# A transformer layer with a mixture of experts: slot table by one-hot matmuls, expert rows added to the residual by accumulating transfers

## The chip, the cores and the metric

The kernel runs on one core of one Trainium2 chip. The metric is the device time of one execution in microseconds (us). Three timed runs of the kernel before gave 2468.05, 2471.11 and 2472.49 us, with a median of 2471.11.

## The reference, cut to what matters

One layer over 2048 latent tokens of width 1024 and 256 context tokens: modulation, a token mixer (recurrence and windowed attention), a residual and layer norm that give `x`, and then the part that the change touches:

```python
h_lat = modulate(x, sh2, sc2).reshape(B * S, D)
y = hier_moe(h_lat, router_g, router_gb, router_e, router_eb, w1, w3, w2)
x = layer_norm(ALPHA * x + g2 * y, ln2_g, ln2_b)

def hier_moe(xf, ...):                         # top-1 of 4 groups, top-2 of its 8 experts
    gate = softmax(top_v) * p_g                # two gates for each token
    flat_e = expert_id.reshape(-1)             # 4096 assignments over 32 experts
    pcounts = (counts + 127) // 128 * 128      # each expert gets whole blocks of 128 slots
    dest = pstarts[sorted_e] + position        # the slot of each assignment
    xb = x_pad[slot_tok].reshape(n_blocks, 128, D)
    yb = (silu(xblk @ w1[e]) * (xblk @ w3[e])) @ w2[e]     # for each block
    return segment_sum(yb[dest] * gate, tok_sorted)
```

Everything is float32. With these inputs 31 experts are used, in 50 blocks.

## The kernel before

The kernel is eight stages, one after the other, each a block of code in which every engine has its own instruction stream, ordered by semaphores; a stage begins when all engines have left the one before. The last four are output (which writes the residual rows `x1_d` and the modulated rows `h2_d` to DRAM), routing, experts and combine.

**Routing** (`phase_route`, from L1395). The router's logits of all 16 token tiles lie in SBUF as 128 x 576. VectorE finds the group and the two experts of each token with `max` and `max_index`, tile by tile (L1433, L1434, L1445, L1446), builds one-hot rows, TensorE sums them to counts and ranks (L1536, L1537), and VectorE derives the slot of each of the 4096 assignments (`slot_i`, L1475), the list of experts in use (L1492) and the tables that steer the expert loop (L1481 to L1511). Each instruction waits for the one before it on a semaphore (`link`). To turn "slot of an assignment" into "token of a slot", GpSimd issues 32 indirect transfers of 128 token numbers each to a DRAM table, `slot_tok_d` (L1547). SyncE then reads the table back (L1563), TensorE transposes it (L1539) and VectorE writes it to SBUF as `gidx`, one column for each block (L1524). SyncE starts the first expert's weights as soon as the expert list is there (L1391).

**Experts** (`phase_experts`, from L1566). For each block of 128 slots: GpSimd copies a column of `gidx` to `ix` (L1642), gathers 128 rows of `h2_d` by an indirect transfer (L1645) and waits until they have landed; TensorE transposes them, multiplies by w1 and w3 and, one block later, by w2 (L1814 to L1816, three half-precision products for each float32 one). For each new expert SyncE loads 6 MB of weights in six pieces of 1 MB through one staging area (L1391), ScalarE rounds each piece to its high half (L1661, L1667) and VectorE subtracts to get its low half (L1734). VectorE scales the block's result by `g2` into the single buffer `y0` (`scale_y`, L1770), and ScalarE stores it to `y_d`, by a transfer placed one step later in its stream (`store_y`, L1688):

```python
def scale_y(n):
    dve.wait_ge(y_mm, START + n + 1)
    dve.wait_ge(y_st, START + 16 * n)      # the store before has landed
```

TensorE's second product of block n waits for `scale_y` of block n - 1. Last, SyncE writes zeros to the unused blocks of `y_d` (L1630).

**Combine** (`phase_combine`, from L1871). For each of the 16 token tiles, with two buffers: GpSimd copies two columns of `slot_i` and gathers the tile's two rows from `y_d` (L1905, L1909); ScalarE multiplies `x1` by ALPHA (L1934, L1939); VectorE adds the two gated rows (L1960, L1961), takes mean and variance (L1962 to L1967), applies the norm in two full-width steps (L1968, L1972) around a `pow` that GpSimd computes (L1915), and ScalarE stores the tile (L1931). VectorE waits for each of its own instructions on a semaphore before the next.

Of the kernel before, what the change touches and what calls it, by code (L numbers as in the profile page):

```python
# [8 lines left out]
F16 = mybir.dt.float16  # L9
# [6 lines left out]
P = 128  # L16
# [25 lines left out]
NG = 4  # L42
# [14 lines left out]
TAB_NB, TAB_NB1, TAB_NB2, TAB_NR, TAB_FREE, TAB_NR1 = 224, 225, 226, 227, 228, 229  # L57
# [14 lines left out]
e_ssv e_pw_s e_a_tr e_o_mm e_o_act e_v e_pw e_h_tr e_h_ev e_r_mm e_lg f_ld f_v f_act f_mm f_tr g_st_ld0  # L72
g_st_ld1 g_st_ld2 g_st_ld3 g_st_ld4 g_st_ld5 g_hi13 g_lo13 g_hi2 g_lo2 g_g2_ld g_x_ix g_x_tr g_x_hi g_x_lo
g_up_mm g_silu g_h g_h_tr g_h_hi g_h_lo g_y_mm g_y_ev g_y_st g_zero g_z_st h_ld h_ix h_v h_pw h_a_x h_mh
h_x_ld0 h_x_ld1 h_o_st0 h_o_st1
# [13 lines left out]
def hybrid_layer(nc, x, c2, w_mod, b_mod, w_in, rg_par, lam, rg_wa, rg_wx, ctx_x, sink, w_out, gn, ln1, router, router_b,  # L89
                 w1, w3, w2, ln2, cos_t, sin_t, ident, masks, tri, iota, tok_id, out):  # L90
    with ExitStack() as stack:
# [20 lines left out]
        x1_d = dram("x1_d", [SEQ, D])  # L112
        h2_d = dram("h2_d", [SEQ, D])
        slot_tok_d = dram("slot_tok_d", [64 * P, 1], I32)
        y_d = dram("y_d", [64 * P, D])
# [4 lines left out]
        slot_i = sb("slot_i", [P, 2 * T_LAT], I32)  # L120
        gates = sb("gates", [P, 2 * T_LAT])
        blk_tab = sb("blk_tab", [1, TAB_SIZE], I32)
        gidx = sb("gidx", [P, 66], I32)
# [48 lines left out]
def phase_modulation(nc, env):  # L172
# [10 lines left out]
    zi = small[0:64, 128:256].bitcast(I32)  # L183
# [5 lines left out]
    with nc.Block() as block:  # L189
        @block.sync  # L190
        def _(sp):
# [15 lines left out]
            sp.wait_ge(rows_st, 32)  # L207
# [31 lines left out]
        def _(dve):  # L239
            nc.vector.memset(zi, 0).then_inc(rows_done, 1)  # L240
# [1154 lines left out]
def phase_route(nc, env):  # L1395
# [5 lines left out]
    names = [("logits", T * 36), ("pad8", T * 8), ("gm8", T * 8), ("gi8", T * 8), ("gif", T), ("goh", T * NG),  # L1401
             ("elm", T * NE), ("em8", T * 8), ("ei8", T * 8), ("eif", 2 * T), ("gex", T * NG), ("gsum", T), ("pg", T),
             ("dif", T), ("q", T), ("oh0", T * NE), ("oh1", T * NE), ("ohs", T * NE), ("base", (T + 1) * NE),
             ("rank", T * NE), ("sel", T * NE), ("slotf", 2 * T), ("nbi", NE), ("nb", NE), ("pend", NE), ("pst", NE),
             ("one32", NE), ("ones", P), ("tri", P), ("iota", 64), ("tok", T), ("ge", 64 * NE), ("has", NE), ("rk", NE), ("rend", NE), ("ebf", 64), ("nw", 64),
             ("st_i", P), ("st_f", P)]
    b = arena_slices(arena, 0, names)
    v3 = lambda name, t, n: b[name].rearrange("p (t n) -> p t n", t=t)
    slot_i, gates, tab, gidx = g["slot_i"], g["gates"], g["blk_tab"], g["gidx"]
    f_ld, v, act_d, mm, scat, tr = sem("f_ld"), sem("f_v"), sem("f_act"), sem("f_mm"), g["plain_sem"]("f_scat"), sem("f_tr")  # L1410
    mark = {}

    with nc.Block() as block:  # L1413
        @block.vector
        def _(dve):
# [11 lines left out]
            link(V.memset(b["pad8"], NEG))  # L1427
            link(V.memset(b["one32"], 1.0))
            link(V.memset(b["ones"], 1.0))
            link(V.memset(b["base"][:, 0:NE], 0.0))  # L1430
            link(V.tensor_copy(v3("pad8", T, 8)[:, :, 0:NG], lg[:, :, 0:NG]))
            for t in range(T):
                link(V.max(v3("gm8", T, 8)[:, t, :], v3("pad8", T, 8)[:, t, :]))  # L1433
                link(V.max_index(v3("gi8", T, 8)[:, t, :].bitcast(U32), v3("gm8", T, 8)[:, t, :], v3("pad8", T, 8)[:, t, :]))  # L1434
            link(V.tensor_copy(b["gif"], v3("gi8", T, 8)[:, :, 0].bitcast(U32)))
            dve.wait_ge(f_ld, START + 48)
# [7 lines left out]
            for t in range(T):  # L1444
                link(V.max(v3("em8", T, 8)[:, t, :], v3("elm", T, NE)[:, t, :]))  # L1445
                link(V.max_index(v3("ei8", T, 8)[:, t, :].bitcast(U32), v3("em8", T, 8)[:, t, :], v3("elm", T, NE)[:, t, :]))  # L1446
# [119 lines left out]
def phase_experts(nc, env):  # L1566
# [38 lines left out]
    with nc.Block() as block:  # L1605
# [49 lines left out]
        def _(act):  # L1655
# [34 lines left out]
            def step(n, prev, stored):  # L1690
# [11 lines left out]
                if stored:  # L1702

                    store_y(n - 2)
# [332 lines left out]
```

## Time and profile before

| | |
|---|---|
| median of three timed runs | 2471.11 us |
| the profiled execution | 2464.56 us |
| its span, first to last instruction | 2462.7 us |
| TensorE busy | 1869.2 us (76%) |
| VectorE busy | 1569.8 us (64%) |
| ScalarE busy | 976.4 us (40%) |
| GpSimd busy | 360.2 us (15%) |
| mean granted TensorE clock | 0.876 |
| moved by transfers | 406.08 MB |

Busy shares are means over stages with different limits. The stages that matter here follow one another and share no work: routing from 1329.3 us, experts from 1416.4, combine from 2316.0 to the end. What one of them loses or gains is read from its own stretch.

### The profile page before, as it was taken

How to read it: one execution, taken by the hardware profiler on the slowest of the kernel's cores; microseconds unless marked ns; L12 is line 12 of the kernel's file. 1: busy time of each engine (PE TensorE's matmuls, PEld its weight loads, DVE VectorE, ACT ScalarE, POOL GpSimd, SP SyncE). 2: the span in 40 equal slices, each digit the busy share in tenths (PEclk: the TensorE clock that was granted, in tenths of full speed). 3: DMA queues.
4: the chain of work that ended last, by engine and by line, in shares of the span. 5: the costliest groups of instructions: out<-in, count | busy, mean ns of one | idle time of the engine just before them, and what ended most of it. 6: DMA issues, size and time to landing. Idle time of an engine off the chain costs nothing. (4 is left out here: it accounts for less than half of the span.)

```text
span 2462.7 us, 42135 instructions
## 1 busy us (share of the span) xinstructions
PE 1869.2 (76%) x12030; PEld 1097.0 (45%) x12031; DVE 1569.8 (64%) x1965; ACT 976.4 (40%) x1253; POOL 360.2 (15%) x346
## 2 busy tenths in 40 slices
PE   6789999953327888699994079999999999999300
PEld 1157676731106777445552034444444444444100
DVE  1355445348887878676776352666668999646387
ACT  2022232245546767522220041445446777434111
POOL 0000000000001121122221510211111211102154
PEclk9989999976668999798896589999999999999755
DMA  9611111011014111123331561777769999939375
GB/s 361 208 40 54 49 43 43 22 35 37 36 51 172 47 54 51 56 103 126 113 122 42 103 214 68 273 264 264 277 252 388 397 399 399 344 141 341 147 254 204
DMA packets 169583, 406.08 MB, mean 165 GB/s; under 512 B 19348, under 2 KB 32052, under 8 KB 168500
## 3 DMA queue, kind: packets, MB, share of 16 engines
q1 hardware_dynamic: 146904, 326.69, 37.0%
q0 software_dynamic: 13120, 44.06, 5.4%
q10 hardware_dynamic: 9504, 34.61, 3.5%
q8 instruction: 32, 0.52, 0.1%
q14 instruction: 23, 0.19, 0.0%
HBM read 329.73 MB, written 75.60 MB: 165 GB/s over the span
## 5 line engine op out<-in xcount | busy, mean ns | idle before, releaser
L1814 PE MATMUL ps<-arena 128*128 x1200 | 457.2, 381 | 33.2 <-DVE arena L1734 32.6
L1734 DVE SCALAR_TENSOR_TENSOR arena<-arena 128x2048 f32 (+1 forms) x186 | 419.2, 2287 | 87.4 <-ACT arena L1667 45.8
L1815 PE MATMUL ps<-arena 128*128 x1200 | 456.6, 380 | 0.0
L1816 PE MATMUL ps<-arena 128*128 x1200 | 456.4, 380 | 0.0
L558 PE MATMUL ps<-arena 128*128 128x256 f16 (+1 forms) x2448 | 325.5, 295 | 21.6 <-DVE arena L469 21.5
L1661 ACT ACTIVATE arena<-arena 128x2048 f32 (+1 forms) x124 | 232.4, 1907 | 164.9 <-PEq L1413 66.0
L558 PEld LDWEIGHTS ps<-arena 128*128 128x128 f16 x2448 | 241.9, 99 | 99.5 <-issue 17.5
L1814 PEld LDWEIGHTS ps<-arena 128*128 128x128 f16 x1200 | 117.7, 98 | 175.4 <-issue 49.1
L1816 PEld LDWEIGHTS ps<-arena 128*128 128x128 f16 x1200 | 117.8, 98 | 139.0 <-issue 2.3
L1815 PEld LDWEIGHTS ps<-arena 128*128 128x128 f16 x1200 | 117.7, 98 | 130.1 <-issue 1.7
L823 PE MATMUL ps<-arena 128*128 128x512 f32 (+1 forms) x160 | 77.2, 648 | 109.0 <-DVE arena L728 71.9
L1642 POOL COPY ix<-gidx 128x1 int32 x52 | 51.3, 986 | 697.7 <-PE ps L1809 545.9
L982 PE MATMUL ps<-arena 128*128 (+3 forms) x768 | 99.4, 268 | 55.7 <-DMA arena<-qT_d 54.5
L1667 ACT ACTIVATE arena<-arena 128x2048 f32 (+1 forms) x62 | 116.1, 1905 | 63.7 <-issue 42.2
L1734 DVE SCALAR_TENSOR_TENSOR arena<-ps,arena 128x512 f16<-128x512 f32 (+1 forms) x101 | 96.5, 955 | 67.9 <-ACT arena L1684 41.5
L994 PE MATMUL ps<-idn,arena 128*128 128x128 f32 x640 | 100.2, 291 | 43.8 <-DVE arena L1046 42.5
L1040 DVE CUSTOM_DVE_ANT_0 arena<-ps,arena,small 128x640 f32<-128x640 f32 x128 | 112.8, 881 | 29.0 <-PE ps L982 17.1
L1082 ACT ACTIVATE arena<-ps 128x640 f16<-128x640 f32 x128 | 90.0, 703 | 76.1 <-PE ps L1013 71.7
L1351 PE MATMUL ps<-arena 128*128 128x512 f16 x256 | 107.3, 419 | 2.9 <-ACT arena L1308 2.9
L1073 ACT ACTIVATE arena<-arena,small 128x640 f32<-128x640 f32 x128 | 104.9, 820 | 6.3 <-DVE small L1040 6.3
L1352 PE MATMUL ps<-arena 128*128 128x512 f16 x256 | 106.6, 416 | 0.0
L994 PEld LDWEIGHTS ps<-idn,arena 128*128 128x128 f32 x640 | 75.7, 150 | 68.3 <-issue 64.3
(247 smaller groups left out, 2969.3 us busy)
## 6 DMA issues: line engine op xcount, KB each, us to landing
arena<-w SPq DMA_DIRECT2D x186, 1024.0 KB
y_d<-arena ACTq DMA_DIRECT2D x50, 512.0 KB, 6.2
arena<-w_mod SPq DMA_DIRECT2D x12, 2048.0 KB, 8.3
arena<-x SPq DMA_DIRECT2D x8, 1024.0 KB, 5.6
arena<-x SPq DMA_DIRECT2D x16, 512.0 KB, 4.5
x_d<-arena SPq DMA_DIRECT2D x16, 512.0 KB, 2.6
h_d<-arena SPq DMA_DIRECT2D x16, 512.0 KB, 3.1
arena<-x_d SPq DMA_DIRECT2D x16, 512.0 KB, 5.4
```

Source lines behind the costliest of these rows:

```text
L558: mm = pe.matmul(o, lhs, rhs, start=first and n == 0, stop=last and n == 2)
L994: mm = pe.transpose(pT(m)[:, q * P:(q + 1) * P], b[f"s{m % 4}"][:, q * P:(q + 1) * P], idn[:])
L1040: nc.vector.tensor_tensor_reduce(b[f"s{m % 4}"], scores_at(m), b[f"mask{j}"], -undo, neg_sink[:, h:h + 1], ALU.add, ALU.min, nm[j][:, h:h ...
L1073: nc.scalar.activation(b[f"s{m % 4}"], b[f"s{m % 4}"], ACT.Exp, bias=nm[j][:, h:h + 1], scale=-1.0, accum_out=den[j][:, h:h + 1]).then_inc ...
L1351: pe.matmul(o, lhs_hi, whi[:, k0 + k, cols], start=(k == 0), stop=False)
L1352: pe.matmul(o, lhs_hi, wlo[:, k0 + k, cols], start=False, stop=False)
L1661: nc.scalar.activation(part(buf, whi, n * PIECE, PIECE), b["st"][:, n * PIECE:(n + 1) * PIECE], ACT.Copy, scale=W_SCALE).then_inc(hi13, 1)
L1667: nc.scalar.activation(part(buf, whi, n * PIECE, PIECE), b["st"][:, n * PIECE:(n + 1) * PIECE], ACT.Copy, scale=W_SCALE).then_inc(hi2, 1)
L1734: return nc.vector.scalar_tensor_tensor(dst, src, scale, high, ALU.mult, ALU.subtract)
L1814: pe.matmul(out, high, part(buf, whi, at, 512), start=first, stop=False)
L1815: pe.matmul(out, high, part(buf, wlo, at, 512), start=False, stop=False)
L1816: return pe.matmul(out, low, part(buf, whi, at, 512), start=False, stop=last)
```

## The change

Four parts. **Modulation**: instead of a 32 KB table, 512 KB of zeros are written behind the last row of each of `h2_d` and `x1_d` (128 rows more each). **Routing**: group and experts are found for all tiles at once, `max_index` gives way to comparing, taking the first hit and comparing again; the expert list comes ahead of the slots; each assignment's slot is split into block (slot // 128) and place (slot % 128), both become half-precision one-hot tables, and TensorE sums place x (block * token) to `gidx`, and place x (block * gate), in a high and a low part, to `gslot`, the gate of each slot. Empty slots point to the spare rows. **Experts**: `scale_y` multiplies by the slot's gate too (and 1/ALPHA), and GpSimd adds the block to `x1_d` by an indirect accumulating transfer; `y_d`, its zero fill and ScalarE's stores are gone. **Combine**: it reads only `x1_d`, four buffers each for input and output, written out without a loop; VectorE measures tile t + 1 before it finishes t, ScalarE applies the norm in one instruction with a bias, VectorE multiplies by the gain, and the last addition is GpSimd's for three tiles of four.

```diff
# phase_modulation
-            sp.dma_start(g["slot_tok_d"].rearrange("(a b) o -> a (b o)", a=64), zi).then_inc(rows_st, 16)
+            for table in (g["h2_d"], g["x1_d"]):
+                sp.dma_start(table[SEQ:SEQ + P, :], spare).then_inc(rows_st, 16)
# phase_route, VectorE
+            dve.wait_ge(f_ld, START + 64)
+            def first_of(dst, hits, tmp, n):
+                link(V.scalar_tensor_tensor(v3(tmp, T, n), v3(hits, T, n), -64.0, io(n).to_broadcast([P, T, n]), ALU.mult, ALU.add))
+                link(V.tensor_reduce(dst, v3(tmp, T, n), AX_X, ALU.min))
+                link(V.tensor_scalar(dst, dst, 64.0, None, ALU.add))
+            for k, top in enumerate(("m1", "m2")):
+                link(V.tensor_reduce(b[top], v3("elm", T, NE), AX_X, ALU.max))
+                link(V.tensor_tensor(v3("ea", T, NE), v3("elm", T, NE), spread(top, NE), ALU.is_equal))
+                first_of(b["ei"], "ea", "eb", NE)
+                link(V.tensor_tensor(by_expert(f"oh{k}"), io(NE).to_broadcast([P, T, NE]), spread("ei", NE), ALU.is_equal))
...
+            link(V.tensor_tensor(h3("block", S), io(64).to_broadcast([P, S, 64]), spread("blkf", 64), ALU.is_equal))
+            link(V.tensor_tensor(h3("who", S), h3("block", S), spread("tokf", 64), ALU.mult))
+            link(V.tensor_tensor(h3("place", S), b["iotap"].rearrange("p (o n) -> p o n", o=1).to_broadcast([P, S, P]),
+                                 spread("posf", P), ALU.is_equal), "placed")
...
+            dve.wait_ge(mm, START + 3)
+            link(V.scalar_tensor_tensor(gidx[:, 0:64], ps[:, 2, 0:64], -1.0, b["gaddr"], ALU.add, ALU.add))
...
+            dve.wait_ge(mm, START + 4)
+            link(V.tensor_scalar(gslot[:], ps[:, 3, 0:64], 1.0 / (GSCALE * W_SCALE * ALPHA), None, ALU.mult))
# TensorE
+            pe.wait_ge(v, START + mark["placed"])
+            for s in range(S):
+                hit = pe.matmul(ps[:, 2, 0:64], h3("place", S)[:, s, :], h3("who", S)[:, s, :], start=(s == 0), stop=(s == S - 1))
+            hit.then_inc(mm, 1)
+            pe.wait_ge(gate_p, START + 12)
+            for s in range(S):
+                pe.matmul(ps[:, 3, 0:64], h3("place", S)[:, s, :], h3("gh", S)[:, s, :], start=(s == 0), stop=False)
+                hit = pe.matmul(ps[:, 3, 0:64], h3("place", S)[:, s, :], h3("gl", S)[:, s, :], start=False, stop=(s == S - 1))
# GpSimd; ten small steps on the gates come ahead of these
+            pool.wait_ge(v, START + mark["placed"])
+            G.tensor_tensor(h3("gh", S), h3("block", S), sp16("ghi16"), ALU.mult).then_inc(gate_p, 1)
+            G.tensor_tensor(h3("gl", S), h3("block", S), sp16("glo16"), ALU.mult).then_inc(gate_p, 1)
-                    pool.indirect_dma_start(g["slot_tok_d"], bass.IndirectOffsetOnAxis(slot_i[:, k * T + t:k * T + t + 1], 0),
-                                            b["tok"][:, t:t + 1].bitcast(I32), None).then_inc(scat, 16)
# phase_experts, GpSimd
+            def scatter(m):
+                pool.wait_ge(y_ev, START + m + 1)
+                if not isinstance(m, int) or m > 0:
+                    pool.wait_ge(y_add, 16 * m)
+                nc.gpsimd.tensor_copy(ix[:, 2:3], gidx[:, bass.ds(m, 1)]).then_inc(y_ix, 1)
+                pool.wait_ge(y_ix, START + m + 1)
+                pool.indirect_dma_start(g["x1_d"], bass.IndirectOffsetOnAxis(ix[:, 2:3], 0), b["y0"], None, compute_op=ALU.add)\
+                    .then_inc(y_add, 16)
+            for n in range(5):
+                gather(n, n % 2)
+            scatter(0)
+            gather(5, 1)
+            scatter(1)
+            gather(6, 0)
+            with pool.Fori(1, (nb >> 1) - 1) as i:
+                scatter(2 * i)
+                gather(2 * i + 5, 1)
+                scatter(2 * i + 1)
+                gather(2 * i + 6, 0)
...
+            pool.wait_ge(y_add, nb * 16)
# VectorE
             def scale_y(n):
                 dve.wait_ge(y_mm, START + n + 1)
-                dve.wait_ge(y_st, START + 16 * n)
+                    dve.wait_ge(y_add, 16 * n)
# phase_combine, GpSimd, ScalarE and VectorE, for tile t
+                nc.gpsimd.tensor_tensor(b[f"rs{j}"], b[f"ve{j}"], b["mh"], ALU.pow).then_inc(pw, 1)
+                if t >= 2 and on_pool(t - 2):
+                    move(t - 2)                       # o += l2b, 128 x 1024; on_pool: t % 4 != 3
...
+                nc.scalar.activation(b[f"o{j}"], b[f"x{j}"], ACT.Identity, bias=b[f"shift{j}"], scale=b[f"rs{j}"]).then_inc(norm_a, 1)
+                if t >= 2:
+                    store(t - 2)
...
+            measure(0)
+            for t in range(T_LAT):
+                if t + 1 < T_LAT:
+                    measure(t + 1)                    # two bn_stats, bn_aggr, + EPS2
+                shift(t)                              # waits for the pow of t
+                if t:
+                    scale(t - 1)                      # o *= l2g; for t - 1 = 3, 7, 11, 15 also o += l2b
+            scale(T_LAT - 1)
```

A gather no longer waits until it has landed, only its reader does; each of the two `x` buffers has its own semaphore.

## Rows read from the trace of the kernel before

**Rows 1.** Windows by stage: us, then busy us (count) of PE, PEld, DVE, ACT, POOL, then clock, DMA share, GB/s.

```profile
100.00:110.00 10.00, 9.90 (x24) 1.78 (x21) 0.68 (x1) 0.00 (x0) 0.00 (x0) 1.00 0.00 0
1430.00:2311.00 881.00, 852.81 (x4200) 422.20 (x4200) 586.65 (x382) 437.71 (x331) 131.50 (x100) 0.99 0.75 280
1865.00:2105.00 240.00, 227.96 (x1124) 112.56 (x1122) 219.10 (x132) 167.11 (x115) 42.05 (x26) 1.00 1.04 397
2315.90:2462.70 146.80, 0.00 (x0) 0.00 (x0) 108.73 (x128) 16.93 (x16) 71.23 (x81) 0.50 0.67 236
```

**Rows 2.** Timeline of the routing stage: start us, us, engine, line, operation, idle before and releaser.

```profile
1329.39 0.17 DVE L1427 MEMSET arena<- 128x128 f32 x1 [0.38 <-PEq L1156]
...
1415.65 0.23 DVE L1524 CAST gidx<-ps 128x64 int32<-128x64 f32 x1 [0.53 <-PE ps L1539]
...
1364.59 2.26 POOL L1547 DMA_INDIRECT slot_tok_d<-arena,slot_i  x1 [43.53 <-DVE blk_tab L1489]
...
1406.13 0.95 POOL L1547 DMA_INDIRECT slot_tok_d<-arena,slot_i  x1 [0.30 <-issue]
...
1368.23 10.60 SPq L1391 DMA_DIRECT2D arena<-w  x6
...
1416.37 0.35 SPq L1608 DMA_DIRECT2D arena<-mod_rows  x1
```

**Rows 3.** Timeline, three VectorE operations of the routing stage.

```profile
1338.74 0.69 DVE L1441 TENSOR_TENSOR arena<-arena 128x512 f32<-128x512 f32 x1
...
1371.16 2.28 DVE L1481 TENSOR_TENSOR arena<-arena 1x2048 f32<-1x2048 f32 x1
...
1377.87 0.22 DVE L1514 TENSOR_REDUCE arena<-arena 128x16 f32<-128x64 f32 x1
```

**Rows 4.** Window of 0.43 us in attention, half-precision 128x64 matmuls (L1011 to L1013).

```profile
901.43:901.86 0.43, 0.43 (x17) 0.42 (x15) 0.16 (x2) 0.43 (x2) 0.20 (x1) 1.00 0.00 0
```

**Rows 5.** Groups of GpSimd instructions over the span: count, busy us, mean ns, idle before.

```profile
L1645 POOL DMA_INDIRECT arena<-h_d,ix x52 | 85.0, 1635 | 42.2 <-POOL ix L1642 42.2
...
L1915 POOL TENSOR_TENSOR arena<-arena 128x1 f32<-128x1 f32 x16 | 25.1, 1567 | 53.0 <-DVE arena L1967 53.0
L962 POOL TENSOR_TENSOR arena<-arena 128x1024 f32 x8 | 18.8, 2346 | 0.0
```

**Rows 6.** Waits in the expert stage: total us, times, longest us.

```profile
ACT arena L1661 <- DMA arena<-w: 34.3, 33, 2.0
...
PE ps L1814 <- DVE arena L1734: 32.6, 23, 8.1
...
DVE arena L1770 <- DMA y_d<-arena: 30.8, 8, 4.8
```

**Rows 7.** DMA issues by line: count, KB each, median us to landing.

```profile
y_d<-arena ACTq DMA_DIRECT2D x50, 512.0 KB, 6.2
```

**Rows 8.** One line's transfers, the gathers of L1645, from issue to landing.

```profile
DMA to landing us min/median/max: 4.0/7.5/11.0
```

**Rows 9.** Timeline, VectorE and GpSimd side by side in the expert stage.

```profile
1966.62 2.28 DVE L1734 SCALAR_TENSOR_TENSOR arena<-arena 128x2048 f32 x1
1966.62 2.32 POOL L1642 COPY ix<-gidx 128x1 int32 x1 [6.35 <-DMA arena<-h_d,ix]
```

**Rows 10.** Timeline of the change from the expert to the combine stage.

```profile
2311.24 1.23 DVE L1770 SCALAR_TENSOR_TENSOR arena<-ps,arena 128x1024 f32<-128x1024 f32 x1 [7.18 <-PE ps L1816]
...
2315.95 0.83 SPq L1888 DMA_DIRECT2D arena<-ln  x2
```

**Rows 11.** Timeline of the combine stage, VectorE.

```profile
2326.82 1.29 DVE L1960 SCALAR_TENSOR_TENSOR arena<-arena,gates 128x1024 f32<-128x1024 f32 x1 [14.36 <-ACT arena L1934]
...
2421.37 0.69 DVE L1962 BATCH_NORM_STATS2 arena<-arena 128x6 f32<-128x512 f32 x1
...
2423.25 1.29 DVE L1968 SCALAR_TENSOR_TENSOR arena<-arena 128x1024 f32<-128x1024 f32 x1
...
2458.32 1.28 DVE L1972 SCALAR_TENSOR_TENSOR arena<-arena 128x1024 f32<-128x1024 f32 x1 [0.50 <-POOL arena L1915]
```

More of the change, by code:

```diff
@@ L182, in phase_modulation @@
     c2a = small[:, 2 * KD:4 * KD]
-    zi = small[0:64, 128:256].bitcast(I32)
+    spare = arena[:, 3 * KD * 512 + 6 * D:3 * KD * 512 + 7 * D]
     wmod_v = g["w_mod"].rearrange("(k p) n -> p k n", p=P)
@@ L1400, in phase_route @@
     T = T_LAT
[L1401 to L1406, printed above, removed]
+    S = 2 * T
@@ L1475, in _ @@
-            link(V.tensor_copy(slot_i[:], b["slotf"]), "slots")
-            one = lambda ap: ap[0:1]
             def count_le(dst, n, limit):
@@ L1533, in _ @@
         def _(pe):
[L1534 to L1539 removed]
+            pe.wait_ge(const, START + 6)
+            pe.wait_ge(act_d, START + 1)
@@ L1545, in _ @@
-            for k in range(2):
-                for t in range(T):
-                    pool.indirect_dma_start(g["slot_tok_d"], bass.IndirectOffsetOnAxis(slot_i[:, k * T + t:k * T + t + 1], 0),
-                                            b["tok"][:, t:t + 1].bitcast(I32), None).then_inc(scat, 16)
-            pool.wait_ge(scat, 16 * 2 * T)
+            G = nc.gpsimd
+            G.memset(half("ones16"), 1.0).then_inc(const, 1)
+            G.memset(b["first"], 1.0).then_inc(const, 1)
+            G.memset(b["one32"], 1.0).then_inc(const, 1)
@@ L1654, in _ @@
+            for j in range(2):
+                pool.wait_ge(x_ld[j], (nb >> 1) * 16 + 32 - 16 * j)
+                pool.sem_inc(g["alone"], 1)
+            pool.wait_ge(y_add, nb * 16)
+            pool.sem_inc(g["alone"], 1)
         @block.scalar
@@ L1912, in rstd @@
[L1912 to L1925 removed]
+            pool.wait_ge(mh_d, START + 1)
@@ L1927, in _ @@
+            for t in range(T_LAT - 2, T_LAT):
+                if on_pool(t):
+                    move(t)
         @block.scalar
         def _(act):
-            def store(i, j):
-                act.wait_ge(v, START + NV * (2 * i + j + 1))
-                act.dma_start(g["out"][bass.ds((2 * i + j) * P, P), :], b[f"o{j}"]).then_inc(o_st[j], 16)
-            for j in range(2):
-                act.wait_ge(x_ld[j], START + 16)
-                nc.scalar.activation(b[f"xa{j}"], b[f"x1{j}"], ACT.Copy, scale=ALPHA).then_inc(a_x, 1)
@@ L1935, in _, with store @@
-            with act.Fori(0, LAST) as i:
-                for j in range(2):
-                    store(i, j)
-                    act.wait_ge(x_ld[j], START + 16 * i + 32)
-                    nc.scalar.activation(b[f"xa{j}"], b[f"x1{j}"], ACT.Copy, scale=ALPHA).then_inc(a_x, 1)
-            for j in range(2):
-                store(LAST, j)
-            for j in range(2):
-                act.wait_ge(o_st[j], START + 16 * (T_LAT // 2))
+            def store(t):
+                j = t % R
+                if on_pool(t):
+                    act.wait_ge(moved, START + t - t // 4 + 1)
+                else:
+                    act.wait_ge(scaled, START + t + 1)
+                act.dma_start(g["out"][t * P:(t + 1) * P, :], b[f"o{j}"]).then_inc(o_st[j], 16)
```

373 lines of the change are left out of this document (191 added, 182 removed).

## The prediction

> **What bounds the kernel now.** I read the page's slices first, then the windows by stage, the timelines of routing and combine, and the waits and transfers of the expert stage. Three stages behave in three ways.
>
> Routing is a chain without a partner. VectorE starts at 1329.39. From 1364.59 to 1406.13 GpSimd issues 32 small transfers, 31 intervals in 41.54 us, 1.34 us each; their landing, a read-back and a transpose follow, and `gidx` is written at 1415.65. The next stage starts at 1416.37 [rows 2]. Nothing else runs but the first expert's weights, issued at 1368.23 and long in.
>
> The expert stage is TensorE's: busy 852.8 of 881 us at a clock of 0.99, 17.6 us for each of the 50 blocks. In one part, 1865 to 2105, transfers bound it: DMA share 1.04 at 397 GB/s [rows 1]. A block with a new expert moves 6.29 MB of weights, 0.52 gathered and 0.52 stored, 7.34 MB; 240 us x 397 GB/s = 95.3 MB is 13 such blocks, 18.5 us each. TensorE's waits for VectorE are 32.6 us in all, ScalarE's for weights 34.3 at one of its two lines, and VectorE's for the y store 30.8 in 8 times [rows 6].
>
> Combine lasts 146.8 us for 16 tiles [rows 1]. From the first tile's start at 2326.82 to the last instruction at 2458.32 less 6.5 us of its own tile's steps, the period is 8.3 us: four full-width steps of 1.29, statistics and waits for `pow` (1.57 us) [rows 5, 11]. TensorE is idle; transfers are at 0.67.
>
> **Part 1, routing.** The start-to-start price of a VectorE step is its duration and some 0.03 us: 0.72 for 128x512, 0.25 for 128x64, 2.3 for 2048 elements in a row [rows 3], 0.2 for the smallest. VectorE now waits first for four constant loads, the fourth issued some 1.3 us after the stage's start and landing some 2 later: start at 1332.6. Groups and masks: nine steps, 2.4. Experts: 6 + 5 steps of 0.72 and two of 0.21, 8.3. Sum of one-hots 0.72, scan 1.1 (taken as half as long again as a plain step), copy 0.22, difference 0.72. "Counted" is at 1332.6 + 13.5 = 1346.1. The counts' matmul and its hand-over take 0.6; three small steps, two on one row, two of 1.24 and one more, 3.9: the expert list is at 1350.6, where it was at about 1367, and the weights start 17 us earlier, which nothing waits for. Reciprocal and prefix 0.9, rank and selection 5 x 0.72, eight small ones 1.4, together 5.9, then the one-hot tables of 2048, 2048 and 4096 columns: 2.2 + 2.2 + 4.3 = 8.7. "Placed" is at 1365.2.
>
> TensorE's 32 + 64 half-precision matmuls of 64 columns: 17 in 0.43 us at the full clock [rows 4], 0.025 us each; the clock is at its low level in routing as the idle 10 us windows show, so I take 0.055: 1.8 and 3.5 us. VectorE, 4.7 us of table steps meanwhile, writes `gidx` at about 1371 and ends the block tables (6.9 us) at 1378. GpSimd, from 1365.2, makes the two gate tables of 2048 columns. Its one wide operation in the trace is 128x1024 at 2.35 us [rows 5]; twice the columns are 4.7, two are 9.4, to 1374.6. But it and VectorE's two-input steps exclude one another (below), some 5 us of such steps: 1379. Then 3.5 of matmuls, 0.3 for `gslot`, 0.7 to the next stage: 1384.4 against 1416.4, **-32 us**. Bounds: -36 if nothing collides, -23 if GpSimd's half-precision products cost twice.
>
> A collision is seen: a GpSimd copy of one column that starts with a two-input VectorE instruction ends with it, 2.32 us beside 2.28 [rows 9]. The Trainium skill ("SBUF — State Buffer", "Who interferes with whom") says why: both use one pair of ports, held for a whole instruction, and the second to come is blocked. By that rule, the trace agrees.
>
> **Part 2, experts.** Removed: 50 ScalarE issues, 14 zero-fills at the end and the y stores. They lie beside TensorE. Added for each block: a copy, an indirect accumulating transfer on GpSimd, and a wait of VectorE for it. Behind that wait on VectorE stand the next block's low halves, for which TensorE waits. The chain from one `scale_y` to the next is: 1.2 for itself, up to 2.3 for a blocked copy [rows 9], 0.8 to the issue (42.2 us of waits for the copy over 52) [rows 5], and the landing. The trace has no accumulating transfer. The nearest rows: the plain store lands in 6.2 (median) [rows 7], the gather, of the same size and queue, in 4.0 to 11.0, median 7.5 [rows 8]. With 7.5 the chain is 11.8, with 11 it is 15.3, both inside 17.6 to 18.5; and it starts directly at `scale_y`, while ScalarE's store came up to a step later. So the new wait is hidden, and of the 30.8 us of the old one I credit 2, for TensorE was mostly busy beside it.
>
> Where transfers are the bound, the added work counts. Adding to DRAM reads the row as well as writing it. From below: it costs as a plain write, 0. From above: three times a write, 2 x 1.32 us x 13 blocks = 34. I take twice: 0.52 MB / 397 GB/s = 1.32 us, x 13 = **+17 us**; less the 2, +15. Zero is no nearer than 34, and the read is real traffic.
>
> The gather no longer holds GpSimd until it has landed. In a block GpSimd needs two copies and two issues, with blocked copies and the mean issue 2 x (2.3 + 0.8 + 1.6) = 9.4 of 17.6 us [rows 5]; the next gather stands behind `scatter`, with one and a half blocks to spare.
>
> The last block: `scale_y` ends at 2312.47 and combine starts 3.5 us later [rows 10]. Now GpSimd copies and issues (1.1) and the addition lands in 4.0 to 7.5: 6.9 on average, **+4** (0 to +8).
>
> The Trainium skill ("SBUF — State Buffer", "Summary: rules for kernel authors") advises against such a move: a transfer issued from GpSimd has its descriptors written by that engine, which VectorE can starve, one from ScalarE has not. The gathers show it, 4.0 to 11.0 [rows 8]. It changes the sum only if the chain outgrows the block, which is the first rival.
>
> **Part 3, combine.** VectorE per tile: measure 1.88 (2421.37 to 2423.25) [rows 11], shift 0.2, one multiplication of 1.3, and for one tile in four another 1.4: 3.75. GpSimd per tile: pow 1.57 and 3/4 of a 2.35 addition [rows 5], 3.3 with waits 3.6. They exclude one another only in the wide steps: the addition of 2.35 starts as a multiplication ends, VectorE measures and shifts for 2.1 beside it and then waits 0.3. ScalarE 16.93 us over 16, 1.06 [rows 1], and an issue. Transfers: 1.05 MB per tile, 2.6 us at 397 GB/s. So 4.1 us per tile, VectorE's. Input has four buffers: a load is issued after the norm and wanted three tiles, 12 us, later. The sum: start, six transfers of 512 KB landing 10 us in (the first tile starts after 10.9 now), first measure 1.9, 16 x 4.1 = 65.6, last scale 2.8, the last store 3.1 as now: 83.4. I take 82: **-65 us**. Bounds: 76 (no waits at all, 3.75 per tile) and 102 (chain of pow, norm, multiplication and addition half exposed, 5.3 per tile): -71 to -45.
>
> **Part 4, modulation.** 1 MB of zeros, 2.6 us at 397 GB/s, is written beside the last weights. From 100 to 110 TensorE is busy 9.9 of 10 us and no transfer runs [rows 1], so it hides: **0**; 2.6 if it delays the last weights.
>
> **The sum.** -32 + 15 + 4 - 65 + 0 = -78. The profiled execution took 2464.56 (span 2462.7 and 1.9 around it): 2386.6. The median of the runs is 6.5 higher: **2393 us**.
>
> **Rivals.**
> - A: the additions pace the expert stage where it is saturated or new experts follow closely. For it: gathers land in up to 11.0 there, and adding rows asks for more; against it: 4.5 us of slack even then. With a landing of 18 the chain is 22.3, 2.5 above the forecast's 19.8, x 13 = 33: 2426 (2405 to 2450). Chance 0.13.
> - B: combine keeps the chain, as VectorE and GpSimd block one another: 5.3 us per tile, 2412. For it: pow, norm, multiplication and addition of one tile are 6.3 us in a row; against it: other tiles lie between. Chance 0.10.
> - C, the other side: each addition runs its 128 rows with read and write one after the other, and all 50 blocks are paced by it. The savings outside the experts are 93 us, 1.9 per block, so it decides from 17.6 + 1.9 = 19.5 us per block, a landing of 17.3 with unblocked copies (19.5 - 1.2 - 0.2 - 0.8). At 18: 50 x 2.6 = 130 more than now, less 93: 2508. For it: no row shows an addition; against it: plain rows of the same size take 4.0 at best. Chance 0.04.
> - D: routing doesn't end earlier than -15, because GpSimd's ten small steps and two tables cost some us more each. Against it: 12 us of room before they are wanted. 2410. Chance 0.05.
> - The forecast: 0.68, 2370 to 2415.
>
> Faster by over 0.2% (5 us, about what a measurement of this kernel can tell from no change): all but C, 0.95; same 0.01; slower 0.04. The range that holds 8 in 10, into A and with the additions' bounds: 2366 to 2432.
>
> **What would show it.** No transfer between "slots" and `gidx`, the expert stage starting near 1384 and GpSimd's gate tables as the last thing before it. A busy expert stage of 1430 to 2311 less 32 with 13 blocks at 19.8 us rather than 18.5, and no TensorE wait traced to `y_add`. Combine of 82 us with VectorE over 85% busy. It is wrong if VectorE's `scale_y` waits for additions in most blocks, or if the tile period in combine is above 4.6.

## The result and the profile after

The changed kernel took 2398.65 us (median of 4 runs, 2395.46 to 2399.96); the kernel before, on the same chip, 2469.74 (4 runs, 2468.05 to 2472.49). The ratio is 0.9709 with a 95% interval of [0.9692, 0.9726]: 71 us, 2.9% faster. Forecast were 2393, in a range of 2366 to 2432. The profiled execution took 2395.46 us, its span is 2393.6.

Windows by stage of the changed kernel, with the columns of [rows 1]: routing, experts, the twelve blocks in a row in which transfers are the bound (called saturated below), the stage change, combine.

```profile
1331.00:1389.00 58.00, 6.53 (x99) 5.33 (x99) 51.19 (x76) 0.67 (x3) 12.04 (x19) 0.53 0.31 111
1389.00:2301.00 912.00, 855.98 (x4208) 424.34 (x4208) 604.04 (x387) 452.09 (x338) 237.14 (x204) 0.98 0.79 266
...
1866.00:2104.00 238.00, 212.28 (x1035) 104.28 (x1034) 198.40 (x117) 154.63 (x106) 75.44 (x48) 0.99 1.01 363
...
2301.00:2314.00 13.00, 0.00 (x0) 0.00 (x0) 0.00 (x0) 0.00 (x0) 1.76 (x2) 0.56 0.27 40
2314.00:2394.00 80.00, 0.00 (x0) 0.00 (x0) 62.18 (x100) 19.90 (x16) 50.60 (x29) 0.50 0.62 223
```

The same twelve blocks of the kernel before:

```profile
1895.00:2114.00 219.00, 207.35 (x1021) 102.43 (x1020) 195.28 (x117) 151.11 (x105) 41.59 (x26) 1.00 1.02 390
```

The reader sees three things. VectorE fills routing (51 of 58 us, where it was idle through most of the 32 transfers before). TensorE's work in the expert stage is the same (856.0 us; 854.9 before, from stage start to the last `scale_y`) in a longer stage. In the saturated blocks the 16 DMA engines are as busy as before (1.01 and 1.02) and move less, 363 GB/s instead of 390, and TensorE is idle for 26 us of them instead of 12.

From stage start to stage start, in us:

| stage | before | after | difference | forecast |
|---|---|---|---|---|
| routing | 87.1 (1329.28 to 1416.37) | 57.4 (1331.43 to 1388.83) | -29.7 | -32 |
| experts, to the end of the last `scale_y` | 896.1 | 912.05 | +16.0 | +15 |
| from there to combine's first load | 3.5 | 13.3 | +9.8 | +4 |
| combine | 146.8 | 79.5 | -67.3 | -65 |
| all ahead of routing | | | +2.1 | 0 |
| sum | 2462.7 | 2393.6 | -69.1 | -78 |

The 26th and the 38th `scale_y` of the 50, first in the kernel before and then in the changed one, show where the expert stage lost:

```profile
1894.79 1.22 DVE L1770 SCALAR_TENSOR_TENSOR arena<-ps,arena 128x1024 f32<-128x1024 f32 x1
...
2113.15 1.22 DVE L1770 SCALAR_TENSOR_TENSOR arena<-ps,arena 128x1024 f32<-128x1024 f32 x1
```

```profile
1865.56 1.28 DVE L1833 SCALAR_TENSOR_TENSOR arena<-ps,gslot,arena 128x1024 f32<-128x1024 f32 x1
...
2103.04 1.28 DVE L1833 SCALAR_TENSOR_TENSOR arena<-ps,gslot,arena 128x1024 f32<-128x1024 f32 x1
```

The twelve blocks between them take 218.4 us before and 237.5 after, 18.20 and 19.79 each: +19.1. Up to the 26th block the changed kernel is 1.7 us ahead of the old one (each counted from its stage's start), and behind the 38th it gets back 1.5.

Waits in the expert stage of the changed kernel, with the columns of [rows 6]:

```profile
ACT arena L1734 <- DMA arena<-w: 63.9, 46, 5.2
...
ACT arena L1740 <- DMA arena<-w: 54.6, 35, 5.5
...
PE ps L1876 <- DVE arena L1796: 47.9, 31, 5.6
...
DVE arena L1833 <- DMA x_d<-arena,ix: 16.3, 4, 4.6
```

VectorE waits for an addition in 4 blocks of 50, 16.3 us, where it waited for the y store in 8, 30.8 us. What grew is the wait for weights: ScalarE's at its two lines was 34.3 and 21.2 us before, 55.5 together, and is 63.9 and 54.6 now, 118.5 together. Behind it stands TensorE's wait for the low halves, which VectorE makes from what ScalarE has rounded: 32.6 us before [rows 6], 47.9 now. These 15.3 us are nearly all of the 16.0 that the stage lost. ScalarE's other line before:

```profile
ACT arena L1667 <- DMA arena<-w: 21.2, 16, 1.9
```

### The profile page after: what moved, and what is told of

It is laid out like the page before. It is cut to its first block and busy times, and to the rows that moved or that the text cites. A ratio compares the mean times of both kernels' runs of the same rounds, so it can differ in the third digit from the quotient of the medians.

```text
span 2393.6 us, 41853 instructions
## 1 busy us (share of the span) xinstructions
PE 1876.9 (78%) x12124; PEld 1103.9 (46%) x12125; DVE 1538.5 (64%) x1840; ACT 982.5 (41%) x1254; POOL 421.3 (18%) x383
## 3 DMA queue, kind: packets, MB, share of 16 engines
HBM read 313.51 MB, written 69.26 MB: 160 GB/s over the span
## 5 line engine op out<-in xcount | busy, mean ns | idle before, releaser
L1876 PE MATMUL ps<-arena 128*128 x1200 | 457.6, 381 | 47.9 <-DVE arena L1796 47.9
L1734 ACT ACTIVATE arena<-arena 128x2048 f32 (+1 forms) x124 | 233.5, 1909 | 148.4 <-DMA arena<-w 63.9
L1740 ACT ACTIVATE arena<-arena 128x2048 f32 (+1 forms) x62 | 117.5, 1909 | 70.7 <-DMA arena<-w 54.6
L1043 DVE SCALAR_TENSOR_TENSOR arena<-ps,arena 128x640 f16<-128x640 f32 x128 | 104.9, 820 | 1.9 <-ACT arena L1079 1.9
```

What stands on the lines that cost most here:

```text
L1734: nc.scalar.activation(part(buf, whi, n * PIECE, PIECE), b["st"][:, n * PIECE:(n + 1) * PIECE], ACT.Copy, scale=W_SCALE).then_inc(hi13, 1)
L1740: nc.scalar.activation(part(buf, whi, n * PIECE, PIECE), b["st"][:, n * PIECE:(n + 1) * PIECE], ACT.Copy, scale=W_SCALE).then_inc(hi2, 1)
L1876: pe.matmul(out, high, part(buf, whi, at, 512), start=first, stop=False)
```

## The experiments

Each number of a run is its ratio to the kernel before, measured on the same chip; the medians of the kernel before were 2466.89 for the first four, 2465.86 for the next four and 2465.66 for the last two. Differences to the changed kernel are therefore taken between ratios, times 2469.74 us, and are uncertain by 5 to 7 us (both intervals taken together); where a difference is smaller, the stages of the profiled executions decide. Of these, routing took 57.0 to 57.4 us in every kernel that has the changed one's tables unaltered, and combine 80.1 to 80.3 in the five experiments that left it alone (e1, e2, e3, e6, e9), 79.5 in the changed kernel.

### The addition taken away: e1_plain

```
-  pool.indirect_dma_start(g["x1_d"], bass.IndirectOffsetOnAxis(ix[:, 2:3], 0), b["y0"], None, compute_op=ALU.add)
+  pool.indirect_dma_start(g["x1_d"], bass.IndirectOffsetOnAxis(ix[:, 2:3], 0), b["y0"], None)
```

> The scatter of each expert block writes its rows over x1_d instead of adding to them (the sum of the two experts and the residual is left out); queue, descriptors, waits and the rest are the changed kernel's. Theory (an addition costs the transfer engines twice a write, 1.3 us more per block): the 13 blocks of the saturated stretch fall from 19.6 us back to about 18.4, the last scatter lands in about 8 us instead of 11, total about 2398 - 16 - 3 = 2380 us. Rival (the cost is that the transfer now goes through GpSimd's queue): the period stays at 19.6 us, total within 3 us of 2398.

Measured: 2372.31 us, ratio 0.9624 [0.9604, 0.9644], 21 us below the changed kernel by the ratios and 23.3 by the spans. The same pair of rows, of this kernel:

```profile
1862.83 1.28 DVE L1833 SCALAR_TENSOR_TENSOR arena<-ps,gslot,arena 128x1024 f32<-128x1024 f32 x1
...
2080.42 1.28 DVE L1833 SCALAR_TENSOR_TENSOR arena<-ps,gslot,arena 128x1024 f32<-128x1024 f32 x1
```

The block takes 18.13 us in the saturated part, what the kernel before needs with its y store. Expected were 18.4 and 2380 us in all. The 23.8 us that the stage got shorter, up to the last `scale_y`, are 19.9 in the twelve saturated blocks and 3.9 in the 38 others; the 3 us expected behind the last one didn't come (13.6 us to the next stage, 13.3 in the changed kernel; section on e9). The window 1900 to 1950 stands at the old rate:

```profile
1900.00:1950.00 50.00, 46.87 (x231) 22.96 (x230) 46.84 (x29) 36.54 (x27) 20.63 (x12) 1.00 1.04 399
```

The queue of GpSimd's transfers, of the changed kernel and then of this one (packets, MB, share of 16 engines over the span):

```profile
q0 software_dynamic: 14832, 54.01, 9.2%
```

```profile
q0 software_dynamic: 14832, 54.01, 6.1%
```

Same packets, same bytes, and 9.2% of 2393.6 is 220 us against 6.1% of 2370.3, 145 us: an addition of 512 KB holds the 16 engines 75 / 50 = 1.5 us longer than the plain scatter. The saturated block grew by 1.66. ScalarE's two waits for weights are 36.0 and 18.9 us, TensorE's for the low halves 26.9. So the addition itself, and not GpSimd's queue, made the expert stage longer, and it does it as time of the 16 engines. (This run also shortens the landing; that the wait for it costs nothing is shown by e3.) The last transfer of the stage has the engines for itself, in the changed kernel and then in this one:

```profile
2304.00:2308.00 4.00, 0.00 (x0) 0.00 (x0) 0.00 (x0) 0.00 (x0) 0.00 (x0) 0.50 0.87 131
```

```profile
2278.00:2282.00 4.00, 0.00 (x0) 0.00 (x0) 0.00 (x0) 0.00 (x0) 0.87 (x1) 0.53 0.32 131
```

The same 131 GB/s over 4 us, 0.52 MB, keep the engines busy for 0.87 x 4 = 3.5 us as an addition and for 1.3 as a plain write.

### The addition made narrow: e2_narrow

```
+  part_d = dram("part_d", [SEQ + P, 32])
-  ... g["x1_d"], bass.IndirectOffsetOnAxis(ix[:, 2:3], 0), b["y0"], None, compute_op=ALU.add)
+  ... g["part_d"], bass.IndirectOffsetOnAxis(ix[:, 2:3], 0), b["y0"][:, 0:32], None, compute_op=ALU.add)
```

> The accumulating scatter moves 32 of the 1024 columns to a small table of its own, so the experts' rows are left out of the result; the number of descriptors, GpSimd's work and all waits stay. Theory (bytes in a saturated stretch are the cost): 6.8 MB per block at 397 GB/s are 17.2 us, so TensorE and VectorE bound the blocks again at about 17.5 us: 13 x 2.1 = 27 us less, and 5 us less at the tail: about 2366 us. Rival (the chain scale_y, copy, issue, landing paces the blocks): about 2398 less only what the landing shortens, above 2385 us.

Measured: 2353.8 us, ratio 0.9554 [0.9532, 0.9576], 38 us below the changed kernel by the ratios and 43.1 by the spans. The pair of rows for it is at 1859.78 and 2063.22, 16.95 us per block, which is TensorE's own time (the window 1900 to 1950, in which the DMA engines are full too):

```profile
1900.00:1950.00 50.00, 50.00 (x251) 24.99 (x250) 49.88 (x30) 38.13 (x27) 21.59 (x13) 1.00 1.05 395
```

With the same instructions and waits on GpSimd and VectorE, and a thirty-second of the added bytes, the stretch is TensorE's to the last tenth, and TensorE's wait for the low halves is 15.0 us in the whole stage. That the order of GpSimd's work costs anything there is refuted. The gain is larger than the expected 32 us, by 6 in the ratios and 11 in the spans. The saturated blocks gave 34.0 us and not 27: they fell to 16.95 us where 17.5 were expected, from 19.79 and not 19.6. The stage change gave 3.1 us and not 5; of the rest 4.1 lie in the other blocks and 2.5 ahead of routing. Of the 2.84 us per saturated block, 1.66 are the addition over a plain write (e1) and 1.18 the plain write itself.

### Two buffers for y: e3_two_y

```
-  ("y0", D)
+  ("y0", 2 * D)
   ...
-  if not isinstance(n, int) or n > 0:
-      dve.wait_ge(y_add, 16 * n)
+  if not isinstance(n, int) or n > 1:
+      dve.wait_ge(y_ix, START + n)
```

and, cut here, `y_of(n)`, one half of `y0` by turns, in `scale_y` and `scatter`, with the last additions written out for it.

> Two y0 buffers: VectorE waits for the scatter before the last one, GpSimd's scatters still follow one another. Theory (the new wait is hidden, 16.3 us of it in 4 places beside TensorE's work): within 4 us of 2398. Rival A (the additions' landing paces saturated blocks through VectorE's wait): 10 us or more below 2398, with the saturated period back under 19 us.

Measured: 2393.33 us, ratio 0.9707 [0.9686, 0.9727], the changed kernel's 0.9709. VectorE's wait for the landing is gone, and what is left of it is GpSimd's:

```profile
POOL ix L1703 <- DMA x_d<-arena,ix: 14.7, 3, 5.3
```

TensorE's wait for the low halves is 44.7 us, against 47.9, and the expert stage takes 924.3 us from start to start, against 925.3. So rival A of the prediction (the landing of the additions paces the stage) is refuted: VectorE's 16.3 us of waits for them were covered.

### The new routing alone: e4_route_alone

The kernel before with the new tables, its transfers of slots gone, and its own y store, gathers and combine stage. The core of the edit is the routing function of the changed kernel with gates and token numbers written for the old stages.

> The kernel before with the new routing stage alone (and the zero rows): y_d, its stores, the gathers of combine and the old combine stay. Theory: routing ends 28 us earlier against its own start and nothing gives it back: 2470 - 28 = 2442 us. Rival (the time is given back in the expert stage, where the first blocks wait for weights or rows): above 2452 us.

Measured: 2438.66 us, ratio 0.9894 [0.9873, 0.9916], 26 to 28 us below the kernel before. Routing takes 57.0 us in its profile, experts 901.9 from stage start to stage start (899.6 before), combine 146.2 (146.8). So routing's gain arrives almost whole, and 2 us of it are given back in the expert stage.

### The combine stage's inputs loaded early: e5_prefetch

The combine stage's own loads of the same six pieces go, and their buffers lie where the expert stage holds nothing (both cut here).

```
   (SyncE, expert stage)
+  for n, name in enumerate(("l2g", "l2b")):
+      sp.dma_start(c[name], g["ln2"][n:n + 1, :].to_broadcast([P, D])).then_inc(sem("h_ld"), 16)
   ...
+  sp.wait_ge(y_add, nb * 16)
+  for t, name in enumerate(COMBINE_X):
+      sp.dma_start(c[f"x{t}"], g["x1_d"][t * P:(t + 1) * P, :]).then_inc(sem(name), 16)
```

> Complete kernel. SyncE loads the two LayerNorm rows of the combine stage at the start of the expert stage, and its first four tiles of x1 after the last addition has landed, ahead of the stage change. In the changed kernel the combine stage began at 2314.1 us and VectorE's first measure at 2324.4, having waited for the LayerNorm rows. Theory (that load wait is on the end's path and nothing else is late there): 8 to 10 us below the changed kernel's 2398.65, so about 2389.5; the first measure within 2 us of the stage's start. Rival (the wait only covers something else, GpSimd's or ScalarE's start of the stage, or the x tiles then come late): within 3 us of 2398.65.

Measured: 2384.62 us, ratio 0.9673 [0.9658, 0.9689], 8.9 us below the changed kernel. VectorE's first measure in the stage, of the changed kernel (stage start 2314.14) and of this one (2314.33):

```profile
2324.43 0.69 DVE L2014 BATCH_NORM_STATS2 arena<-arena 128x6 f32<-128x512 f32 x1 [23.55 <-DMA arena<-ln]
```

```profile
2314.44 0.69 DVE L2025 BATCH_NORM_STATS2 arena<-arena 128x6 f32<-128x512 f32 x1 [13.41 <-PEq L1662]
```

Ten microseconds of landing at the start of a stage were on the end's path, all of them: combine takes 69.3 us instead of 79.5. (The expert stage took 2.7 us more in this execution, 928.0; with the same early loads it is 0.5 more in e8 and 1.4 less in e10, so that is not the loads' cost.) The x1 tiles could be loaded ahead of the stage change because the last addition lands 5.7 us ahead of it (SyncE issues the loads at 2308.66).

### Gate tables on ScalarE: e6_act_gates

```
-  G.tensor_tensor(h3("gh", S), h3("block", S), sp16("ghi16"), ALU.mult).then_inc(gate_p, 1)
-  G.tensor_tensor(h3("gl", S), h3("block", S), sp16("glo16"), ALU.mult).then_inc(gate_p, 1)
+  for s in range(S):
+      for dst, src in (("gh", "ghi"), ("gl", "glo")):
+          nc.scalar.activation(h3(dst, S)[:, s, :], h3("block", S)[:, s, :], ACT.Copy, scale=b[src][:, s:s + 1])
   ...
```

> Complete kernel. The two gate tables of the routing stage are made by 64 ScalarE steps of 128x64 out of the block table, in place of GpSimd's two multiplications of 3.60 us. Beside those two, VectorE's 1x32 steps took 3.39 us (0.17 elsewhere) and 4.57 us (1.21 elsewhere). Theory (VectorE's chain sets the end of routing, and GpSimd's two multiplications hold it up): 3.2 + 3.4 = 6.6 us come back, 2392. Rival (the gate products, then waiting for 64 ScalarE steps of about 0.2 us, or the strided steps set the end, whoever makes the tables): within 2 us of 2398.65, or above it.

Measured: 2389.94 us, ratio 0.969 [0.9675, 0.9705], 4.7 us below the changed kernel; routing takes 51.1 us instead of 57.4, -6.3. The timeline of routing in the changed kernel, with the columns of [rows 2]:

```profile
1365.10 4.42 DVE L1509 TENSOR_TENSOR arena<-arena 128x4096 f16<-128x4096 f32 x1
...
1369.67 3.60 POOL L1601 TENSOR_TENSOR arena<-arena 128x2048 f16<-128x2048 f16 x1 [13.97 <-DVE arena L1509]
1373.23 3.60 POOL L1602 TENSOR_TENSOR arena<-arena 128x2048 f16<-128x2048 f16 x1
...
1369.91 3.39 DVE L1514 TENSOR_SCALAR arena<-arena 1x32 f32<-1x32 f32 x1
1373.34 4.57 DVE L1480 TENSOR_TENSOR arena<-arena 1x1024 f32<-1x1024 f32 x1
...
1380.96 0.22 DVE L1523 SCALAR_TENSOR_TENSOR gidx<-ps,arena 128x64 int32<-128x64 f32 x1
...
1388.11 0.23 DVE L1539 TENSOR_SCALAR gslot<-ps 128x64 f32<-128x64 f32 x1
```

The same two VectorE steps and the stage's last, while ScalarE makes the tables and GpSimd is silent:

```profile
1371.73 0.17 DVE L1514 TENSOR_SCALAR arena<-arena 1x32 f32<-1x32 f32 x1
1371.93 1.21 DVE L1480 TENSOR_TENSOR arena<-arena 1x1024 f32<-1x1024 f32 x1
...
1383.61 0.23 DVE L1539 TENSOR_SCALAR gslot<-ps 128x64 f32<-128x64 f32 x1 [0.29 <-PE ps L1570]
```

A step of 32 elements in one partition took 3.39 us because a GpSimd operation was in progress: the two steps end 0.03 us after GpSimd's first and 1.08 after its second, and without GpSimd they take 0.17 and 1.21. The chain that ends routing is VectorE's, with that block in it. ScalarE's 64 steps took 15.37 us (0.334 at the median, not 0.2), and VectorE's last step waited 0.29 us behind them: a little longer, and they would have set the end.

### Combine without GpSimd's additions: e7_all_dve

```
   def on_pool(t):
-      return t % 4 != 3
+      return False
```

> Complete kernel. In the combine stage VectorE does the multiplication and the addition of the LayerNorm rows for all 16 tiles; GpSimd keeps only the power step of each. Theory (after the change GpSimd's 1.53 + 2.34 us bound three tiles of four, 3.9 us a tile on the average; VectorE alone needs its measures of about 1.9 and two full-tile steps of 1.22 to 1.25, 4.35): 16 x 0.45 = 7 us slower than 2398.65, less about 2 for the last tiles whose steps are no longer blocked by a GpSimd addition: 2404. Rival (the blocking of VectorE by GpSimd's additions is the cost, a step of 1.22 becoming 2.02 and the last two 3.23): not slower than 2398.65, down to 2392.

Measured: 2396.29 us, ratio 0.9719 [0.9705, 0.9734], 2.5 us above the changed kernel; combine takes 82.5 us in the profile, +3.1 (+2.3 against the five experiments with the changed kernel's combine). The two wide steps, groups of lines of this kernel in its combine stage (count, busy us, mean ns, idle before):

```profile
L2035 DVE TENSOR_TENSOR arena<-arena 128x1024 f32<-128x1024 f32 x16 | 19.6, 1227 | 0.5
L2033 DVE TENSOR_TENSOR arena<-arena 128x1024 f32<-128x1024 f32 x16 | 19.5, 1217 | 0.0
```

All 32 take their 1.22, the tile 4.26 (first `L2033` at 2326.35, the next at 2330.61). In the changed kernel:

```profile
2332.89 2.02 DVE L2031 TENSOR_TENSOR arena<-arena 128x1024 f32<-128x1024 f32 x1
...
2333.79 1.53 POOL L1978 TENSOR_TENSOR arena<-arena 128x1 f32<-128x1 f32 x1
...
2335.29 2.34 POOL L1973 TENSOR_TENSOR arena<-arena 128x1024 f32<-128x1024 f32 x1
...
2382.42 2.34 POOL L1973 TENSOR_TENSOR arena<-arena 128x1024 f32<-128x1024 f32 x1
...
2382.62 3.23 DVE L2031 TENSOR_TENSOR arena<-arena 128x1024 f32<-128x1024 f32 x1
2385.77 1.21 DVE L2033 TENSOR_TENSOR arena<-arena 128x1024 f32<-128x1024 f32 x1
2386.03 3.15 POOL L1973 TENSOR_TENSOR arena<-arena 128x1024 f32<-128x1024 f32 x1 [1.26 <-DVE arena L2031]
2387.01 3.24 DVE L2035 TENSOR_TENSOR arena<-arena 128x1024 f32<-128x1024 f32 x1
```

Four tiles take 15.66 us in the changed kernel (the multiplications at 2329.89 and 2345.55), 3.91 each. For three of them GpSimd goes from `pow` to addition without a gap (3.80 us for 1.53 + 2.34), and a multiplication beside it takes 2.02; in the fourth, whose addition is VectorE's, GpSimd waits 2.77 us. So the theory holds in direction; its 5 us were 3, between both. Sharing an addition with an engine that blocks the other is worth 0.35 us a tile here, less about 3 us at the end of the stage, where the last tiles' steps of 1.2 take 3.2 beside a GpSimd addition.

### The three together: e8_best

The edits of e5 and e6, and GpSimd adds the row only for tiles 0 to 12 (`return t % 4 != 3 and t < 13`).

> Complete kernel: the early loads of the combine stage and ScalarE's gate tables together, and GpSimd adds the LayerNorm row only for tiles before the 13th, so that nothing of it stands beside the last tiles. Theory (the three are on one path, one behind another): 9 + 6.6 + about 3 = 18 to 19 us below 2398.65, 2380. Rival (one of them is covered once another goes): 2385 to 2392.

Measured: 2376.68 us, ratio 0.9638 [0.9625, 0.9652], 17.5 us below the changed kernel; the spans give 19.9. Routing 50.8, combine 67.0 (-12.4, of which -10.2 are e5's), experts 925.8 (925.3). The three add up, being on one path; the third was not run by itself, and its 2.2 us are what e5 leaves of the difference.

### GpSimd's drain: e9_drain and e10_best2

The end of the expert stage in the changed kernel: the last `scale_y`, the last addition, and in a second fence GpSimd's drain (count, duration in ns min/median/max, start). The next stage's first instruction is at 2314.14.

```profile
2299.60 1.28 DVE L1833 SCALAR_TENSOR_TENSOR arena<-ps,gslot,arena 128x1024 f32<-128x1024 f32 x1 [7.54 <-PE ps L1878]
...
2302.32 1.58 POOL L1704 DMA_INDIRECT x_d<-arena,ix  x1 [0.84 <-POOL ix L1700]
```

```profile
L1655 POOLq DRAIN  x1: 5332/5332/5332, 2308.6 to 2308.6; - x1
```

The addition lands 6.3 us after its issue, at 2308.6, and then GpSimd drains for 5.33 us. In the kernel before, GpSimd's last transfer was a gather; its drain of 4.30 us began at 2286.7 and was over before the last `scale_y`.

```
   (end of GpSimd's program in the expert stage)
-  pool.wait_ge(y_add, nb * 16)
   (end of SyncE's)
+  sp.wait_ge(y_add, nb * 16)
```

e10_best2 has the same edit on top of e8_best's.

> Complete kernel. The end of the expert stage alone: the wait for the last addition's landing is SyncE's and not GpSimd's, so that GpSimd reaches its drain when it has issued the last addition. In the changed kernel the last addition was issued at 2302.32 us, landed at 2308.6, and GpSimd's drain took the 5.33 us behind that. Theory (the drain has a length of its own and runs beside the transfer): 5.3 us less, 2393.3, and the next stage starts at the landing. Rival (the drain lasts until the transfer is done and some us more, whoever waits): within 1 us of 2398.65, with a drain of 10 us or more in the trace.

> Complete kernel: the early loads of the combine stage, ScalarE's gate tables and no GpSimd addition beside the last tiles, as in the run before last, and the last addition's wait on SyncE. Theory: 5.3 us below that kernel's 2376.68, 2371.4, since SyncE's four loads of x1 (2.1 us to issue and land beyond the landing) stand behind the same wait and are the next thing late, at the worst 2373.5. Rival (GpSimd's drain waits for the transfer): 2376 to 2377.5.

Measured: e9 2392.74 us, ratio 0.9707 [0.9694, 0.9721], the changed kernel's 0.9709; e10 2374.49, ratio 0.9627 [0.9614, 0.964], against e8's 0.9638, within the intervals. The drain of e9, and then of e1, where the scatter only overwrites:

```profile
L1655 POOLq DRAIN  x1: 10803/10803/10803, 2304.7 to 2304.7; - x1
```

```profile
L1655 POOLq DRAIN  x1: 8477/8477/8477, 2281.3 to 2281.3; - x1
```

From the issue of the last transfer to the end of the drain it is 11.6 us in the changed kernel (2302.32 to 2313.9), 11.1 in e9 (2304.40 to 2315.5), 10.4 in e10 (2295.02 to 2305.4), and 11.9 in e1, whose transfer had landed after 3.4 us. The drain of e2, whose addition has 16 KB, and of the kernel before, behind a gather issued at 2282.39:

```profile
L1656 POOLq DRAIN  x1: 5332/5332/5332, 2264.7 to 2264.7; - x1
```

```profile
L1605 POOLq DRAIN  x1: 4297/4297/4297, 2286.7 to 2286.7; - x1
```

Where GpSimd first waits for the landing of an addition, the drain takes 5.33 us, in the changed kernel and in e2, e3, e5, e6, e7 and e8, whether the landing came after 6.2 to 6.5 us (512 KB) or after 3.2 (16 KB). So the theory had a length right and the overlap wrong: begun 5 us earlier, the drain lasts 5 us longer and doesn't run beside the transfer. The rival's reading, until the transfer is done and some us more, fits e9 and e10: their next stage begins 11.3 and 10.7 us after the issue, where the six kernels with the wait and 512 KB need 11.8 to 12.1, so that about 1 us is won, too little for the times to tell. But its "some us" are no constant: 5.33 behind an addition, 4.30 behind the gather, 8.48 behind e1's overwriting scatter. What GpSimd does in that time the trace doesn't say, and it stays open. The loss is the same in all of them: with GpSimd's last scatter at a stage's end, the next stage begins 8.7 (e2) to 12.1 us after it is issued.

## Why the prediction was right, and where it was off

- **Routing, -32 forecast, -29.7 measured.** The chain was read rightly up to the tables: `experts` at 1353.59 and the weights at 1354.80. VectorE began 3.3 us after the stage's start, as counted. Six steps with a strided operand took 1.01 us where 0.69 was assumed, 2 us in all, and the place table 4.42 (forecast 4.3). What failed is the step "GpSimd's tables end at 1379, then 3.5 of matmuls, then `gslot`": the tables took 3.60 each and not 4.7, TensorE's 64 products, 0.053 us apart, had all started by 1380.24, and the end was VectorE's own chain of small tables, 6.6 us late because GpSimd had blocked two of its steps. The collision was in the forecast, 5 us, but on GpSimd's side; e6 shows on whose side it cost: 6.3 us.
- **Experts, +15 forecast, +16 measured.** The mechanism is shown: the DMA engines are full, weights come later, and TensorE waits 15.3 us more for the low halves; e1 takes it away. That the block measured 19.79 us where 19.8 were forecast is luck: the block before was 18.20 and not 18.5, and the growth 1.59 and not 1.32. The term was 1.32 x 13 = 17, the rows give 1.59 x 12 = 19.1; the 2 us credited for the old wait came as 3.2 in the other blocks, so that the two misses nearly cancel. The reason given (a second pass over the row, at the rate of the transfers) is near the 1.5 us of engine time more per addition, and below the 2.2 more of the last one alone; that it is a read of the row is not shown: the HBM read in the profile is 313.51 MB with the additions and the same 313.51 without them (e1), so their reads are not in that count.
- **The new wait is hidden.** 4 waits, 16.3 us; without them (e3) the time is the same. The landing's size was not the matter: the chain had its slack.
- **The last block, +4 forecast, +9.8 measured.** The mis-sized term. Copy, issue and landing came near the forecast: 7.7 us from the end of the last `scale_y` to the landing, with 6.9 forecast. The forecast ended there, and took the stage change behind a landing as free, as it was after the y store of [rows 10]. What stands there instead is GpSimd's drain, 5.3 us, which was hidden before and isn't now; with it the term lies outside its own bounds of 0 to +8.
- **Combine, -65 forecast, -67.3 measured.** 79.5 us against 82; the tile 3.91 against 4.1. But it was put down to VectorE, and GpSimd is the bound of three tiles in four; VectorE is busy 62.2 of 79.5 us, 78% and not the "over 85%" of the forecast. The 10 us of landing at the start were in the sum (10.3 measured); e5 shows that they needn't be. No run splits the 67 us between the gathers that went and the stage's new order.
- **Modulation, 0.** The stage's last store is issued at 111.81 us, at 110.76 before; in e5, with the same zeros written, at 110.80, in e1 at 111.67. So 0 to 1 us, which the executions don't tell from nothing. Routing began 2.1 us later in this execution; in the ten experiments, whose stages ahead of it are the changed kernel's, it began between 1328.29 and 1334.06, with 1329.28 before: the spread between executions is larger than the term.
- **The sum.** -78 against -69.1 in the profiled pair: +5.8 for the last block, +2.3 for routing, +1 for experts, +2.1 ahead of routing, -2.3 for combine. Of the rivals, A is refuted by e3, B by the tile of 3.91, C by 4 waits of 50 and blocks of 16.8 us outside the saturated part, D by routing's 57.4 us and e4's -26 to -28.

The rule of the Trainium skill ("SBUF — State Buffer", "Who interferes with whom") on which the forecast leaned, two engines that exclude each other for whole instructions, is what the rows of e6 and e7 show, 0.17 becoming 3.39 us. The advice of the Trainium skill ("SBUF — State Buffer", "Summary: rules for kernel authors") against transfers issued from GpSimd found no price inside the stage: without VectorE's wait for them the time is the same (e3), and the gathers land in 3.8/7.3/9.6 us (least, median, most), with [rows 8] at 4.0/7.5/11.0. No run here has the additions issued elsewhere. Nor is it shown that the spread of [rows 8] comes from VectorE, as the prediction read it: no run separates that from full DMA engines.

## What to carry to other kernels

Where transfers bound a stretch, count an accumulating transfer as two to three plain ones of its size in engine time (1.5 us more per 512 KB on average here, 2.2 more for one alone); elsewhere it cost 0.1 us a block, and a combine stage that gathered the rows again could do without them. When a transfer becomes the last thing before a stage change, price what the engine that issued it does at the end of its program too, and look for loads of the next stage that can go ahead of the change: here the two were 5 and 10 us. Before giving an engine's work to another, look which of them block each other, and put the blocked one's short chain where the other is silent.

## What the runs showed of the hardware that was not expected

- An accumulating indirect transfer of 512 KB holds the 16 engines 1.5 us longer than the overwriting one on average (same packets and bytes), 3.5 us instead of 1.3 when alone, and its issue takes 1.59 us on GpSimd at the median, against 0.99; with 16 KB it is 1.59 too. Whatever bytes it reads don't appear in the HBM count.
- GpSimd's drain at the end of a stage takes 5.33 us behind the landing of an addition of 512 or of 16 KB, 8.48 behind an overwriting scatter and 4.30 behind a gather; begun ahead of the landing it ends no more than about 1 us sooner.
- A VectorE step of 1x32 with one input took 3.39 us instead of 0.17 beside a GpSimd multiplication of 3.60.
- GpSimd multiplies 128x2048 half-precision elements in 3.60 us and adds 128x1024 full-precision ones in 2.34: per element a quarter less.
